# Late products with the low part of h, memory tokens scaled by ScalarE, and h of the next norm made during the last output unit

## The chip, the cores and the metric

The kernel runs on one core of one Trainium2 chip. The metric is the device time of one execution in microseconds (us). Before the change the median of three runs is 2518.27 us.

## The reference, cut to what matters

One decoder layer, for 1024 tokens of width 1024:

```python
x = x + 0.5 * swiglu(rmsnorm(x, g1), w_gu1, w_down1)          # FFN 1
h = rmsnorm(x, g_mix)
q_sb, k_sb, v_sb, q_d, k_d, v_d, q_x, gates = split(h @ w_in)
mn = rmsnorm(mem, g_mem);  mk, mv = split(mn @ w_mem_kv)      # 256 memory tokens
o_sb, o_dil, o_x = stick_breaking(...), dilated(...), memory_attention(q_x, mk, mv)
merged = g0 * (o_sb @ w_br_sb) + g1 * (o_dil @ w_br_dil) + g2 * (o_x @ w_br_x)
x = x + merged @ w_out
x = x + 0.5 * swiglu(rmsnorm(x, g2), w_gu2, w_down2)          # FFN 2
```

The norm is y = x * rsqrt(mean(x*x) + eps) * gain. All in float32.

## The kernel before, in words

Activations lie transposed: feature on the partition, token on the free axis, in eight tiles of 128 features by 1024 tokens (`xT`, `h_hi`, `h_lo`). Every large product is made in three parts. A factor is split in a rounded high part and the rest: `h = h_hi + h_lo`, `w = w_hi + w_lo`. The product is `w_hi*h_hi + w_hi*h_lo + w_lo*h_hi`, and that of the two rests is left out.

Weights come as 196 "units" of 128x1024 in a fixed order. SP (line 459) loads a unit into one of two `raw` buffers, ScalarE copies it into `w_hi` (`split_hi`, line 519, instruction at L525), VectorE makes `w_lo` (`split_lo`, line 818, instruction at L823). There are three slots for split weights, so a unit is split up to two units ahead. The semaphores `hi_done` and `split_done` count these two steps, `unit_done` counts units that TensorE has used up.

A unit of a product over eight k tiles is `product` (line 1279): per k, and for both halves of 512 tokens, six matmuls of 128x512, four with `w_hi` and two with `w_lo`, 48 in all. With `there` it waits before each k for that tile of h. Before that wait is over, none of the six is issued.

h is made without the norm's factor: `gain_hi` on ScalarE (line 534, L536) writes `h_hi[k] = gain * xT[k]`, `gain_lo` on VectorE (line 827, L830) the rest, and the factor (`rB`) is applied when PSUM is read. For it ScalarE squares each tile (`square`, L532), GpSimd adds the squares up (L476), `norm_sum` (line 1357) sums over the partitions on TensorE, ScalarE takes Ln, Exp and Square (`rstd`, line 538), and VectorE does a Newton step (`newton_rstd`, line 834). Only then can `ffn_gate` (L851) read the first unit out of PSUM.

The order on each engine is written out by hand. The places that the change touches:

- **First stage** (lines 1426 to 1447 on TensorE, 613 to 627 on ScalarE, 989 to 1000 on VectorE). TensorE turns x tile by tile (`turn_x`, L1423), VectorE takes it out of PSUM (L987), h is made, and the first two units run side by side, tile after tile. After tile 5 VectorE scales the two blocks of memory tokens (L1000). In the iteration of the last k TensorE turns the memory tokens (L1437), VectorE puts them into `mT` (L1004), ScalarE makes `mT_hi` (L631) and VectorE `mT_lo` (L1008). `norm_sum(0)` waits for the last `mT`, as it writes the same banks of PSUM.
- **Units 4 and 7** (`gate_or_up` at lines 1459 to 1468), cut into pieces with the memory products between.
- **Entry of the projections** (line 1515), the first unit behind FFN 1.
- **Output units** (lines 1684 to 1690; L1267 on VectorE adds a finished one to x; h here is `merged`, whose rest is made at L1208 and whose high part at L792).
- **Entry of FFN 2**: ScalarE waits at line 800 until the last output unit is done and then makes all `h_hi` (lines 801 to 805), VectorE makes all `h_lo` after its last addition (line 1268), and the first unit is at line 1346.

```python
act.wait_ge(unit_done, U_OUT + DT)      # line 800
...
for m in range(DT):                     # line 1264
    split_lo(U_OUT + m + AHEAD)
    dve.wait_ge(unit_done, U_OUT + m + 1)
    nc.vector.tensor_tensor(xT[:, m, :], x_back[:, m, :], ps[:, 2 + m % 2, :], ALU.add).then_inc(x_added, 1)
for k in range(DT):
    gain_lo(2, k, 2)
```

## Time and profile before

| | us |
|---|---|
| three runs, median (lowest, highest) | 2518.27 (2513.20, 2518.75) |
| the profiled execution, its own time | 2513.74 |
| its span in the profile | 2511.90 |
| TensorE (PE) busy | 2447.6, 97% |
| VectorE (DVE) busy | 1169.4, 47% |
| ScalarE (ACT) busy | 573.8, 23% |
| GpSimd (POOL) busy | 193.6, 8% |
| mean granted TensorE clock | 0.987 of full speed |
| share of the chain that ended last: PE, DVE, ACT | 92%, 4%, 2% |

PE busy includes the time in which one matmul drains while the next already runs, so it is not a measure of work done at peak. What a stall costs is read from the idle time before an instruction and from what ended it, and what the clock costs from the granted clock of a stretch. Times in the timeline are us from the start of the span.

### The profile page before, as it was taken

Reading aid. Unit: us, or ns where it says so; the run is one execution under the profiler, and the core shown is the slowest. Engines: PE = TensorE matmul, PEld = TensorE weight load, DVE = VectorE, ACT = ScalarE, POOL = GpSimd, SP = SyncE. Lnnn points to the kernel's source line nnn. Section 1 sums busy time; section 2 is a strip of 40 time slices with the busy share of each in tenths; the row PEclk is TensorE's granted clock in tenths of the full one; section 3 lists DMA queues with packets and bytes.
Section 4 is the critical chain, followed back from the end, with each engine's and each line's share of the span. In section 5 each row is a group of like instructions: output and inputs, shape, how many; then the busy total and the mean of one; then the engine's idle time right before and its main releaser. Section 6 shows DMA issues by size and latency. Waiting matters only on the chain.

```text
span 2511.9 us, 25983 instructions
## 1 busy us (share of the span) xinstructions
PE 2447.6 (97%) x10608; PEld 1915.8 (76%) x10608; DVE 1169.4 (47%) x1193; ACT 573.8 (23%) x716; POOL 193.6 (8%) x153
## 2 busy tenths in 40 slices
PE   7999999999999999889999999999999999999998
PEld 6788888888877655446667888878788888888887
DVE  7444444444446666555632533343544444444444
ACT  5211111111114444433413311121301111111111
POOL 2000000000002454330000000001000000000000
PEclk9999999999999999999999999999999999999999
DMA  4211111111113000001012211122111111111112
GB/s 148 73 42 51 50 50 50 42 50 50 50 53 120 26 9 17 17 12 39 26 28 25 59 51 51 51 91 77 42 42 51 50 50 50 42 50 50 50 50 67
DMA packets 48946, 125.80 MB, mean 50 GB/s; under 512 B 4269, under 2 KB 22605, under 8 KB 48624
## 3 DMA queue, kind: packets, MB, share of 16 engines
q1 hardware_dynamic: 45760, 112.69, 14.8%
q10 hardware_dynamic: 2640, 11.08, 1.2%
q0 software_dynamic: 480, 1.10, 0.3%
q8 instruction: 48, 0.79, 0.1%
q14 instruction: 18, 0.15, 0.0%
HBM read 116.42 MB, written 9.87 MB: 50 GB/s over the span
## 4 chain that ended last, share of the span: by engine, by line
PE 92%; DVE 4%; ACT 2%; issue 1%; DMA 0%; SPq 0%; ACTq 0%; DVEq 0%
PE ps L1277 91%; DVE h_lo L830 1%; DVE w_lo L823 0%; PE ps L1616 0%; ACT pr_x L590 0%; ACT pr_x L592 0%; DVE xT L892 0%; PE ps L1563 0%; DMA x_nat<-in_x 0%; DVE d_qk L960 0%; DVE pr_x L952 0%; DVE d_qk L955 0%; DVE h_lo L1208 0%; ACT pr_x L594 0%; PE ps L1405 0%
## 5 line engine op out<-in xcount | busy, mean ns | idle before, releaser
L1277 PE MATMUL ps<-h_hi,w_hi 128*128 128x512 f32 x2240 | 894.1, 399 | 15.7 <-DVE h_lo L830 6.6
L1277 PE MATMUL ps<-h_lo,w_hi 128*128 128x512 f32 x2240 | 878.3, 392 | 0.0
L1277 PE MATMUL ps<-h_hi,w_lo 128*128 128x512 f32 x2240 | 695.2, 392 | 0.0
L1277 PEld LDWEIGHTS ps<-h_hi,w_hi 128*128 128x128 f32 x2240 | 423.6, 189 | 136.7 <-issue 40.5
L1277 PEld LDWEIGHTS ps<-h_hi,w_lo 128*128 128x128 f32 x2240 | 423.0, 189 | 89.7
L1277 PEld LDWEIGHTS ps<-h_lo,w_hi 128*128 128x128 f32 x2240 | 424.2, 189 | 85.4 <-issue 1.9
L525 ACT ACTIVATE w_hi<-raw 128x1024 fp32r<-128x1024 f32 x196 | 204.2, 1051 | 825.6 <-PE ps L1277 799.7
L823 DVE TENSOR_TENSOR w_lo<-raw,w_hi 128x1024 fp32r<-128x1024 f32 x196 | 254.3, 1305 | 154.1 <-ACT w_hi L525 144.4
L892 DVE TENSOR_TENSOR xT<-xT,ps 128x1024 f32<-128x1024 f32 x176 | 214.7, 1220 | 182.7 <-PE ps L1277 182.7
L1277 PE MATMUL ps<-a_hi,w_hi 128*128 128x512 f32 x704 | 276.6, 393 | 5.7 <-DVE w_lo L823 4.9
L1277 PE MATMUL ps<-a_lo,w_hi 128*128 128x512 f32 x704 | 275.6, 391 | 0.0
L1277 PE MATMUL ps<-a_hi,w_lo 128*128 128x512 f32 x704 | 218.1, 391 | 0.0
L858 DVE SCALAR_TENSOR_TENSOR glu<-ps,rB 128x1024 f32<-128x1024 f32 x44 | 53.9, 1224 | 262.4 <-PE ps L1277 262.4
L851 DVE TENSOR_TENSOR silu<-ps,rB 128x1024 f32<-128x1024 f32 x44 | 53.9, 1224 | 252.1 <-PE ps L1277 252.1
L1277 PEld LDWEIGHTS ps<-a_hi,w_hi 128*128 128x128 f32 x704 | 133.0, 189 | 35.1 <-DVE w_lo L823 5.7
L1277 PEld LDWEIGHTS ps<-a_hi,w_lo 128*128 128x128 f32 x704 | 132.8, 189 | 27.8
L1277 PEld LDWEIGHTS ps<-a_lo,w_hi 128*128 128x128 f32 x704 | 133.1, 189 | 27.4
L556 ACT ACTIVATE silu<-silu 128x1024 f32<-128x1024 f32 x44 | 46.6, 1060 | 439.7 <-DVE silu L851 439.7
L476 POOL TENSOR_TENSOR acc<-acc,sq 128x1024 f32<-128x1024 f32 x21 | 51.3, 2442 | 1108.0 <-ACT sq L532 1108.0
L1150 DVE TENSOR_TENSOR gate<-ps,rB 128x1024 f32<-128x1024 f32 x24 | 29.4, 1225 | 126.5 <-PE ps L1277 126.5
L1277 PE MATMUL ps<-sb_q,sb_k 64*128 64x512 f32 (+2 forms) x144 | 62.5, 542 | 17.4 <-ACT sb_a L697 16.0
L760 ACT ACTIVATE gate<-gate 128x1024 f32<-128x1024 f32 x24 | 25.0, 1057 | 172.7 <-DVE gate L1150 172.6
(186 smaller groups left out, 1786.1 us busy)
## 6 DMA issues: line engine op xcount, KB each, us to landing
raw<-in_weights SPq DMA_DIRECT2D x196, 512.0 KB, 3.6
x_nat<-in_x SPq DMA_DIRECT2D x8, 512.0 KB, 7.4
x_keep<-xT ACTq DMA_DIRECT2D x1, 4096.0 KB, 12.6
x_back<-x_keep ACTq DMA_DIRECT2D x1, 4096.0 KB, 12.2
out<-y_nat SPq DMA_DIRECT2D x8, 512.0 KB, 3.3
toe_keep<-toe_row ACTq DMA_DIRECT2D x2, 704.0 KB, 6.6
m_nat<-in_mem SPq DMA_DIRECT2D x1, 1024.0 KB, 8.2
d_fB<-d_f_keep POOLq DMA_DIRECT2D x2, 512.0 KB, 7.3
```

What stands on the lines that cost most here:

```text
L476: nc.gpsimd.tensor_tensor(acc[:], acc[:], sq[:, k % 2, :], ALU.add).then_inc(acc_done, 1)
L525: nc.scalar.activation(w_hi[:, k % NW].rearrange("p a b -> p (a b)"), raw[:, k % NRAW, :], ACT.Copy).then_inc(hi_done, 1)
L556: nc.scalar.activation(silu[:, t % 2, :], silu[:, t % 2, :], ACT.Silu).then_inc(silu_done, 1)
L760: nc.scalar.activation(gate_tile(m, b), gate_tile(m, b), ACT.Sigmoid).then_inc(gate_done, 1)
L823: nc.vector.tensor_tensor(w_lo[:, k % NW].rearrange("p a b -> p (a b)"), raw[:, k % NRAW, :], w_hi[:, k % NW].rearrange("p a b -> p (a b)" ...
L830: nc.vector.scalar_tensor_tensor(out=h_lo[:, k, :], in0=xT[:, k, :], scalar=g32[:, gain, k:k + 1], in1=h_hi[:, k, :].bitcast(F32), op0=ALU ...
L851: nc.vector.tensor_tensor(silu[:, t % 2, :], ps[:, 0, :], rB[:], ALU.mult).then_inc(gate_scaled, 1)
L858: nc.vector.scalar_tensor_tensor(out=glu[:, t % 2, :], in0=ps[:, 1, :], scalar=0.5, in1=rB[:], op0=ALU.mult, op1=ALU.mult).then_inc(up_sca ...
L892: nc.vector.tensor_tensor(xT[:, m, :], xT[:, m, :], ps[:, 2 + m % 2, :], ALU.add).then_inc(down_added, 1)
L1150: nc.vector.tensor_tensor(gate_tile(m, b), ps[:, merge_pair(m, b), :], rB[:], ALU.mult).then_inc(mg_taken, 1)
L1277: return pe.matmul(o, a, b, start=start, stop=stop, skip_group_check=True)
```

## The change

- In the first unit of a stage, products with `h_lo` are no longer issued tile by tile with the others. A new `streamed` waits per k for `h_hi` alone, issues the four matmuls with `h_hi`, and issues the two with `h_lo` of k - 2 after them. It takes the place of `product` with `there` in the first unit of the projections, in the first output unit and in the first unit of FFN 2.
- In the first stage the wait for `h_hi` moves ahead of `turn_x(k + 2)`, the eight matmuls with `h_hi` come before the wait for `h_lo`, and for k = 0 part of them come before the turn of the third x tile. ScalarE splits weight unit 1 before it squares tile 0.
- Units 4 and 7 (`gate_or_up_part`) wait for `hi_done` only, issue what needs `w_hi`, then wait for `split_done` and issue what needs `w_lo`.
- The memory tokens are scaled by ScalarE after tile 6, no longer by VectorE after tile 5.
- In the last output unit each k but the last increments a new semaphore `out_read` as soon as its matmuls are through. ScalarE makes `h_hi[k]` of the next norm as soon as `out_read` allows, VectorE makes `h_lo[0..4]` before it waits for that unit, and `h_lo[5..7]` after its addition. The last square comes before the eighth `h_hi`, no longer before the fourth.

```diff
@@ ScalarE, first stage
                 gain_hi(k, 0)
-                square(0, k)
                 if k == 0:
                     split_hi(1)
+                square(0, k)
...
+                if k == 6:
+                    act.wait_ge(m_rs_done, 2)
+                    for b in range(MB):
+                        nc.scalar.activation(m_nat[:, b, :], m_nat[:, b, :], ACT.Copy, scale=m_rs[:, b:b + 1]).then_inc(m_scaled, 1)
@@ ScalarE, entry of FFN 2
-            act.wait_ge(unit_done, U_OUT + DT)
             for k in range(DT):
-                if k == 3:
+                if k < DT - 1:
+                    act.wait_ge(out_read, k + 1)
+                else:
                     act.wait_ge(x_added, DT)
                     square(2, DT - 1)
                 gain_hi(k, 2)
@@ VectorE, first stage
-                if k == 5:
-                    dve.wait_ge(m_rs_done, 2)
-                    for b in range(MB):
-                        nc.vector.tensor_scalar(m_nat[:, b, :], m_nat[:, b, :], m_rs[:, b:b + 1], None, ALU.mult).then_inc(m_scaled, 1)
@@ VectorE, output units
-                dve.wait_ge(unit_done, U_OUT + m + 1)
+                if m < DT - 1:
+                    dve.wait_ge(unit_done, U_OUT + m + 1)
+                if m == DT - 1:
+                    for k in range(5):
+                        gain_lo(2, k, 2)
+                    dve.wait_ge(unit_done, U_OUT + m + 1)
                 nc.vector.tensor_tensor(xT[:, m, :], x_back[:, m, :], ps[:, 2 + m % 2, :], ALU.add).then_inc(x_added, 1)
-            for k in range(DT):
+            for k in range(5, DT):
                 gain_lo(2, k, 2)
@@ TensorE, new helpers
+            def high_high(pair, slot, k):
+                for c in (0, 512):
+                    mm(ps[:, pair, c:c + 512], w_hi[:, slot, k, :], h_hi[:, k, c:c + 512], k == 0, False)
+            def rest_high(pair, slot, k, final=False):
+                for c in (0, 512):
+                    last = mm(ps[:, pair, c:c + 512], w_lo[:, slot, k, :], h_hi[:, k, c:c + 512], False, final)
+                return last
+            def high_rest(pair, slot, k, final=False):
+                for c in (0, 512):
+                    last = mm(ps[:, pair, c:c + 512], w_hi[:, slot, k, :], h_lo[:, k, c:c + 512], False, final)
+                return last
+            def streamed(pair, slot, hi_done_of, lo_done_of, base):
+                for k in range(DT + 2):
+                    if k < DT:
+                        pe.wait_ge(hi_done_of, base + k + 1)
+                        high_high(pair, slot, k)
+                        rest_high(pair, slot, k)
+                    if k >= 2:
+                        pe.wait_ge(lo_done_of, base + k - 1)
+                        last = high_rest(pair, slot, k - 2, k == DT + 1)
+                return last
...
+            def gate_or_up_part(part, k, t, k0, k1):
+                if k0 == 0:
+                    pe.wait_ge(hi_done, k + 1)
+                    after(pe, (gate_scaled, up_scaled)[part], t)
+                for j in range(k0, k1):
+                    high_high(part, k % NW, j)
+                    high_rest(part, k % NW, j)
+                if k0 == 0:
+                    pe.wait_ge(split_done, k + 1)
+                for j in range(k0, k1):
+                    last = rest_high(part, k % NW, j, j == DT - 1)
@@ TensorE, first stage
             for k in range(DT):
+                pe.wait_ge(h_hi_done, k + 1)
+                if k == 0:
+                    pe.wait_ge(hi_done, 1)
+                    high_high(0, 0, 0)
+                    pe.wait_ge(split_done, 1)
+                    rest_high(0, 0, 0)
                 if k + 2 < DT:
                     turn_x(k + 2)
...
+                if k == 0:
+                    pe.wait_ge(hi_done, 2)
+                    high_high(1, 1, 0)
+                    pe.wait_ge(split_done, 2)
+                    rest_high(1, 1, 0)
+                else:
+                    for part in range(2):
+                        high_high(part, part, k)
+                    for part in range(2):
+                        rest_high(part, part, k)
                 pe.wait_ge(h_ready, k + 1)
                 for part in range(2):
-                    if k == 0:
-                        pe.wait_ge(split_done, part + 1)
-                    last = product(part, part, hh, hl, S, k0=k, k1=k + 1)
+                    last = high_rest(part, part, k, k == DT - 1)
@@ TensorE, output units
-                product(2 + m % 2, u % NW, hh, hl, S, there=(lambda k: pe.wait_ge(mg_split, k + 1)) if m == 0 else None
-                        ).then_inc(unit_done, 1)
+                if m == 0:
+                    last = streamed(2, u % NW, mg_hi_done, mg_split, 0)
+                else:
+                    last = product(2 + m % 2, u % NW, hh, hl, S, read=out_read if m == DT - 1 else None)
+                last.then_inc(unit_done, 1)
```

## Rows read from the trace of the kernel before

**Rows 1.** The page, busy us (share of the span) and instructions of each engine.

```profile
PE 2447.6 (97%) x10608; PEld 1915.8 (76%) x10608; DVE 1169.4 (47%) x1193; ACT 573.8 (23%) x716; POOL 193.6 (8%) x153
```

**Rows 2.** Waits of PE, whole span: waited for, us in total, times, longest.

```profile
PE ps L1277 <- DVE w_lo L823: 8.3, 4, 2.4
PE ps L1277 <- DVE h_lo L830: 6.6, 3, 2.7
PE ps L1277 <- DVE h_lo L1208: 2.2, 1, 2.2
```

**Rows 3.** Stretches: us, busy (x) of PE, PEld, DVE, ACT, POOL, granted clock, DMA.

```profile
40.00:45.00 5.00, 5.00 (x20) 3.99 (x20) 3.72 (x2) 1.59 (x2) 2.53 (x1) 0.66 0.00 0
60.00:90.00 30.00, 28.89 (x143) 24.50 (x144) 14.79 (x22) 10.21 (x12) 0.00 (x0) 0.94 0.30 94
785.00:812.00 27.00, 25.17 (x106) 19.85 (x106) 10.83 (x10) 7.11 (x7) 0.00 (x0) 1.00 0.61 233
1689.00:1701.00 12.00, 12.00 (x47) 9.62 (x46) 2.42 (x3) 2.23 (x2) 0.00 (x0) 0.86 0.73 314
1771.00:1784.00 13.00, 11.94 (x46) 9.58 (x47) 11.05 (x8) 7.82 (x8) 2.87 (x1) 0.87 0.01 1
```

**Rows 4.** Timeline, first stage: start, us, engine, instructions [idle before, releaser].

```profile
29.56 1.03 PE L1423 MATMUL ps<-cst,x_nat 128*128 128x128 f32 x8
30.42 2.41 POOL L476 TENSOR_TENSOR acc<-acc,sq 128x1024 f32<-128x1024 f32 x1 [1.20 <-ACT sq L532]
31.77 2.14 DVE L830 SCALAR_TENSOR_TENSOR h_lo<-xT,g,h_hi 128x1024 fp32r<-128x1024 f32 x1
33.22 1.04 PE L1423 MATMUL ps<-cst,x_nat 128*128 128x128 f32 x8
33.83 3.54 DVE L1000 TENSOR_SCALAR m_nat<-m_nat,small 128x1024 f32<-128x1024 f32 x2
...
38.55 1.15 ACT L536 ACTIVATE h_hi<-xT,g 128x1024 fp32r<-128x1024 f32 x1 [4.56 <-DVE xT L987]
...
39.76 0.50 PE L1277 MATMUL ps<-h_hi,w_hi 128*128 128x512 f32 x1 [2.74 <-DVE h_lo L830]
```

**Rows 5.** Timeline, from the memory tokens to unit 4.

```profile
41.63 2.70 DVE L823 TENSOR_TENSOR w_lo<-raw,w_hi 128x1024 fp32r<-128x1024 f32 x1 [0.61 <-ACT w_hi L525]
...
45.30 3.23 DVE L1004 TENSOR_SCALAR mT<-ps,g 128x256 f32<-128x256 f32 x8 [0.97 <-PE ps L1437]
...
50.06 0.68 PE L1277 MATMUL ps<-mT_hi,w_hi 128*128 128x256 f32 x1
...
57.71 1.22 DVE L851 TENSOR_TENSOR silu<-ps,rB 128x1024 f32<-128x1024 f32 x1
...
60.12 0.50 PE L1277 MATMUL ps<-h_hi,w_hi 128*128 128x512 f32 x1 [2.42 <-DVE w_lo L823]
```

**Rows 6.** Timeline, start of unit 7.

```profile
77.25 0.50 PE L1277 MATMUL ps<-h_hi,w_hi 128*128 128x512 f32 x1 [1.00 <-DVE w_lo L823]
```

**Rows 7.** Timeline, last k of the first projection unit.

```profile
785.80 0.50 PE L1277 MATMUL ps<-h_hi,w_hi 128*128 128x512 f32 x1 [1.18 <-DVE h_lo L830]
```

**Rows 8.** Timeline, seventh k of the first output unit.

```profile
1687.82 1.06 ACT L792 ACTIVATE h_hi<-merged 128x1024 fp32r<-128x1024 f32 x1 [7.75 <-DVE merged L1229]
1688.60 0.50 PE L1277 MATMUL ps<-h_hi,w_hi 128*128 128x512 f32 x1 [2.16 <-DVE h_lo L1208]
```

**Rows 9.** Timeline, last output unit and entry of FFN 2.

```profile
1758.57 1.22 DVE L1267 TENSOR_TENSOR xT<-x_back,ps 128x1024 f32<-128x1024 f32 x1 [5.01 <-PE ps L1277]
...
1761.86 2.57 DVE L823 TENSOR_TENSOR w_lo<-raw,w_hi 128x1024 fp32r<-128x1024 f32 x1 [2.07 <-ACT w_hi L525]
...
1769.45 3.23 ACT L536 ACTIVATE h_hi<-xT,g 128x1024 fp32r<-128x1024 f32 x3 [7.62 <-PE ps L1277]
...
1772.06 0.76 PE L1277 MATMUL ps<-h_hi,w_hi 128*128 128x512 f32 x1 [2.65 <-DVE h_lo L830]
...
1784.64 1.88 PE L1277 MATMUL ps<-acc,cst 128*128 128x512 f32 x4
```

More of the change, by code:

```diff
@@ L340, in layer @@
         br_done = sem("br_done")
-        mg_hi_done, mg_split = sem("mg_hi_done"), sem("mg_split")
+        mg_hi_done, mg_split, out_read = sem("mg_hi_done"), sem("mg_split"), sem("out_read")
         x_added = sem("x_added")
@@ L1277, in mm, with product @@
                 return pe.matmul(o, a, b, start=start, stop=stop, skip_group_check=True)
-            def product(pair, slot, hi, lo, width, tiles=DT, w0=0, there=None, k0=0, k1=None):
+            def product(pair, slot, hi, lo, width, tiles=DT, w0=0, there=None, k0=0, k1=None, read=None):
                 halves = [(c, min(c + 512, width)) for c in range(0, width, 512)]
@@ L1290, in product @@
                         last = mm(ps[:, pair, c:d], w_lo[:, slot, w0 + k, :], hi(k)[:, c:d], False, final)
+                    if read is not None and k < tiles - 1:
+                        last.then_inc(read, 1)
+                return last
[19 more added lines that the diff above has]
+                        last = high_rest(pair, slot, k - 2, k == DT + 1)
                 return last
@@ L1345, in ffn @@
                 if f:
-                    gate_up(u0, t0, there=lambda k: pe.wait_ge(h_ready, 8 * r + k + 1), between=lambda: norm_sum(r))
+                    gate_up(u0, t0, between=lambda: norm_sum(r))
                     for q in range(1, GT):
@@ L1382, in proj @@
                         pe.wait_ge(pr_final, aux_before(before))
+                if n == PR_SB:
+                    streamed(proj_pair(n), proj_unit(n) % NW, h_hi_done, h_ready, 8).then_inc(unit_done, 1)
+                    return
                 last = product(proj_pair(n), proj_unit(n) % NW, hi, lo, w, there=there, k0=k0, k1=k1)
@@ L1406, in proj_aux, with projections @@
                     last.then_inc(pr_aux, 1)
-            def projections(n0, n1, hi, lo, there=None):
+            def projections(n0, n1, hi, lo):
                 for n in range(n0, n1):
-                    proj(n, hi, lo, there if n == n0 else None)
+                    proj(n, hi, lo)
                     if n == n0:
@@ L1513, in sb_values @@
                 last.then_inc(sb_av, 1)
-            projections(PR_SB, PR_BESIDE, hh, hl, lambda k: pe.wait_ge(h_ready, 8 + k + 1))
+            projections(PR_SB, PR_BESIDE, hh, hl)
             pe.wait_ge(pr_copied, PR_BESIDE)
```

26 lines of the change are left out of this document (15 added, 11 removed).

## The prediction

> **What bounds the kernel now.** I read the busy times first: TensorE is busy 97% of the span, no other engine over 47% [rows 1]. So time is only to be had where TensorE stands, or where it runs at half its clock. The view of its waits shows where it stands. Most lie in the attention stages, which the change leaves alone. Three groups are its targets [rows 2]: 6.6 us for `h_lo` of the norms in three waits, 2.2 us for that of the merged tiles in one, and 8.3 us for `w_lo` in four, of which two (2.42 and 1.00) belong to units 4 and 7 [rows 5, 6].
>
> The third view is the clock by stretch [rows 3]. 40 to 45 us has 0.66, 60 to 90 us 0.94, 1689 to 1701 us 0.86, 1771 to 1784 us 0.87. Length times what is missing from 1.00 gives 1.70, 1.8, 1.68 and 1.69 us: each is one stretch of about 3.4 us at 1.2 instead of 2.4 GHz, which costs 1.7 us. Before each TensorE had stood idle: 2.74, 2.42, 2.16 and 2.65 us [rows 4, 5, 8, 9]. After the idle 1.18 us of rows 7 the clock stayed at 1.00. So a stall of over 2 us costs its length plus 1.7 us, one of 1.2 us only its length. That is the price list of this prediction.
>
> The pace of matmuls at full clock: an output unit is 48 matmuls and runs from 1758.5 to 1769.4 us [rows 9] (both ends are marked by what PE released), 10.9 us or 0.227 us each, 1.36 us per k.
>
> **The first stage, up to the norm's sum.** From turn to turn TensorE takes 3.66 us (29.56 to 33.22) [rows 4], all busy. Then VectorE spends 3.54 us on the memory tokens, its second scaling held up by GpSimd's addition, as the subtraction at 31.77 is (2.14 us for some 1.2, ending 1.1 us after GpSimd's 30.42 + 2.41). `h_lo` 6 is late, and TensorE stands 2.74 us and then loses 1.70.
>
> ScalarE takes the scaling over: two Copies of 128x1024, of which a row with a scale costs 1.08 us (3.23 for three) [rows 9], so 2.1 us. It stood idle 4.56 us for the last x tile here [rows 4], so they are hidden; they push `h_hi` 7 to about 37 us, which TensorE wants at 38. Bounds: 0 and 2.1 us, taken as 0. No DMA is issued or moved; SP and GpSimd keep their order.
>
> VectorE now goes straight to x tile 7 (its turn ends at 33.22 + 1.04; 34.3 to 35.5), is held by GpSimd until 36.5 (one period of 3.66 after 30.42 + 2.41), ends `h_lo` 6 at 37.6 and 7 at 38.8. GpSimd's last sum then runs to 41.2 and holds `w_lo` of unit 2 to 42.2 (before: to 44.3) [rows 5]. The eight `mT` follow, 3.23 us, to 45.5. The earlier start (four matmuls move into the wait for the third x tile) may take 0.5 off this, nothing to 1.2. I take 45.3, against 48.5 before, with the norm's sum right behind it and the first memory product 1.5 us behind it (50.06) [rows 5]. **Gain 3.2 us.**
>
> TensorE's own work is done sooner than that: the turn of tile 7 began at 33.22, k = 6 would follow at 36.9, and two k (5.4 us) and sixteen turns (1.9) end at 44.2, or at 42.7 with a start that is 1.5 us earlier. The old stall of 2.74 us and its slow clock are gone, but a new one stands before the sum, of 1.2 to 2.7 us, for `mT`. I take the upper half and so a new slow stretch over the memory products: **-1.6 us** (bounds 0 and 1.7), of which nothing is hidden since memory product 0 and `rstd` end together before.
>
> **Units 4 and 7.** The chain from memory product to `rB` keeps its length. Unit 4 now needs PSUM bank 0 free, which is when L851 ends, 58.93, and no longer `w_lo`, which came at 60.1. Start 58.95 against 60.12: **1.2 us**. The stall is 1.2 instead of 2.42 us, so the clock should hold: **1.7 us**. `w_lo` is wanted 16 matmuls (3.6 us) later and is there. Unit 7 waited 1.00 us for its `w_lo`; its first eight matmuls (1.8 us) now cover that: **1.0 us** (bounds 0, if `w_hi` isn't there either, and 1.0).
>
> **Entry of the projections.** The last k waited 1.18 us for `h_lo` 7 [rows 7]. `h_hi` 7 is long there, and two matmuls are left instead of six when `h_lo` 7 arrives. The seven k before the stall took 9.5 us, so the unit began at 775.1; 46 matmuls end at 785.5, two more after 785.8. End 786.3 against 787.2: **0.9 us**. No clock was lost here.
>
> **First output unit.** Before, TensorE stood at k = 6 for `h_lo` 6 from 1686.4 to 1688.6, with 12 matmuls left (2.72 us): end 1691.3 at full clock. Now it gets through k = 6 and `h_lo` 4 (38 matmuls, 8.6 us from 1678.3) at 1686.9, and then stands for `h_hi` 7, which ends at 1688.88 [rows 8]. Ten matmuls are left, 2.27 us: end 1691.2. The stall is 2.0 us, hardly shorter, the slow stretch stays. **0.1 us.**
>
> **Entry of FFN 2.** Before, TensorE stands from 1769.4 to 1772.06, runs slowly, and reaches the norm's sum at 1784.64 [rows 9]. Now ScalarE, idle 7.62 us there, starts after its split at 1761.8: seven `h_hi` at 1.08 are done by 1769.6, none held long by `out_read` (k = 6 is read at 1768.1). VectorE is free at 1764.4, makes five `h_lo` to 1770.5 and adds tile 7 by 1771.7, 1 us later than before. ScalarE squares it to 1772.8 and has `h_hi` 7 at 1773.9; GpSimd sums to 1775.2; `h_lo` 6, held by it, ends at 1776.4, `h_lo` 7 at 1777.6. TensorE starts at 1769.45, wants `h_hi` 7 at 1778.1 and `h_lo` 7 at 1779.9. Nothing is late, the unit ends at 1769.45 + 10.9 = 1780.35. **4.3 us**, which holds the stall, the slow stretch and 0 to 0.1 of small waits. What is queued behind ScalarE's new waits is only its own h and `rstd`, and that starts with the sum.
>
> By the Trainium skill, page "TensorE: Matmul & The Clock Gate", section "The cost: per-tile semaphore tail", each semaphore increment on a matmul adds about 26 ns. The seven of `out_read` would then take an estimated 0.2 us off the sum. No row here shows such a step.
>
> **Sum.** 3.2 - 1.6 + 1.2 + 1.7 + 1.0 + 0.9 + 0.1 + 4.3 = **10.8 us**. Between the stages TensorE is the bound, so gains are carried on. The profiled execution took 2513.74 us (span 2511.90, 1.84 around it) and would take 2502.9. It lies 4.5 us under the median of 2518.27; from that the forecast is **2507.5 us**.
>
> **Rivals.**
> 1. *More clock than I take.* The new stall before the norm's sum is short (lower end 1.2 us), or the slow stretch at the first output unit doesn't come. Gain 12.4, with both 14.1: 2505.9 to 2504.2. For: the stall's lower end. Against: four of four idles over 2.1 us were followed by a slow stretch. Chance 0.20.
> 2. *The memory chain keeps its old time.* `mT` isn't earlier, for instance because GpSimd and VectorE hold each other up once more, 2.4 us. Then the first term is 0.8 and the sum 8.4: 2509.9. For: it hangs on three turns of GpSimd and VectorE whose order I worked out to half a microsecond. Chance 0.15.
> 3. *The last addition is late.* Five `h_lo` ahead of it, each possibly held to 2.14 us as in rows 4, would bring it to 1776 and the norm's sum to wait; of the 4.3 us some 1.5 would be left, sum 8.0: 2510.3. Against: GpSimd only adds squares there, and that of tile 7 comes after the addition. Chance 0.07.
> 4. *The new order of matmuls is slower.* The old order puts two after each other into one PSUM bank; the new ones change the bank with each matmul. It concerns 336 matmuls. If each ran at half clock, it would cost 0.2 us, 67 us in all, and the time would be about 2574; from 79 such matmuls (10.8 + 5.0 us at 0.2) the change is slower by over 0.2%. Against: a third of today's matmuls (those with `w_lo`) already change bank each time, and 785 to 812 us has clock 1.00 [rows 3]. Chance 0.04. The Trainium skill has a rule for it, page "TensorE: Matmul & The Clock Gate", section "A second HAM failure mode: psum-queue depth-cycling": cycling through banks leaves small idles that make the clock swing between its levels. The trace does not agree so far.
> 5. *Little comes of it*: 2 and 3 together, and a stall that only moved at unit 4, sum 3 to 5 us: about 2514. Chance 0.09.
>
> **How the numbers follow.** My own case has 0.45. About 0.2% (5.0 us) is what a measurement of this kernel can tell from no change. Cases 0 to 3 are faster by more: 0.87; case 5 the same: 0.09; case 4 slower: 0.04. Low end of the range: case 1 with a median that falls among the quicker of the runs (before, 2513.20 to 2518.75): 2500. High end: rivals 2 and 3 with a microsecond more: 2513. The predicted time is that of my case.
>
> **What would show it.** L1000 gone from VectorE, two more ScalarE Copies of about 1.1 us near 34 us. `mT` begun at 42.2 instead of 45.3, and a PE wait for `mT` L1004. Unit 4 released by L851, not L823, and clock 1.00 over the gate products of unit 4. No wait for `w_lo` at unit 7. A wait for `h_lo` L830 of at most 0.4 us at the projections. A wait of about 2.0 us for `h_hi` L792 and still a slow stretch at the first output unit. At FFN 2 no wait and no slow stretch, and 10.9 instead of 15.2 us from the end of the last output unit to the norm's sum. I would be wrong if TensorE's waits for h and `w_lo` shrank as told and the span did not, or if the stretches with the new order took over 0.227 us a matmul.

## The result, and the profile after

| | before | after |
|---|---|---|
| median, us | 2517.06 (2513.20 to 2518.75, 6 runs) | 2498.10 (2495.66 to 2500.43, 6 runs) |
| ratio, 95% interval | | 0.9926 (0.9913 to 0.9939) |
| profiled execution, us | 2513.74 | 2497.57 |
| its span, us | 2511.94 | 2495.67 |

The change gained 19.0 us by the medians, 16.2 us by the two profiled executions. The forecast was 10.8 us and a time of 2507.5, with a range from 2500.0: sign right, size too small, range missed.

The page after the change, engines:

```profile
PE 2439.7 (98%) x10608; PEld 1910.5 (77%) x10608; DVE 1168.8 (47%) x1191; ACT 576.0 (23%) x718; POOL 194.2 (8%) x153
```

The same 10608 matmuls, two instructions fewer on VectorE and two more on ScalarE [rows 1]. PE is busy 7.9 us less with the same work. Most of that is clock: the trace after has four stretches at half clock (1.2 instead of 2.4 GHz) fewer, at 1.7 us each. The other 8.4 us of the gain are waiting. After, the waits of PE that answer to those of before:

```profile
PE ps L1283 <- DVE w_lo L828: 5.1, 3, 2.5
...
PE ps L1283 <- ACT h_hi L796: 2.0, 1, 2.0
...
PE ps L1283 <- DVE silu L856: 1.4, 1, 1.4
PE ps L1283 <- DVE mT L1005: 1.4, 1, 1.4
...
PE ps L1283 <- DVE h_lo L835: 0.3, 1, 0.3
```

17.1 us of waiting [rows 2] became 10.2, and the x DMA at the very start costs 1.5 us less (7.6 after). The stretches that answer to [rows 3] (us, busy and instructions of PE, PEld, DVE, ACT, POOL, granted clock, DMA share, GB/s):

```profile
40.00:45.00 5.00, 3.65 (x15) 2.27 (x13) 5.00 (x15) 4.11 (x9) 0.00 (x0) 1.00 0.38 105
60.00:90.00 30.00, 30.00 (x156) 24.12 (x155) 16.52 (x22) 8.85 (x10) 0.00 (x0) 1.00 0.28 80
1678.00:1690.00 12.00, 11.11 (x42) 9.02 (x43) 2.14 (x3) 3.17 (x3) 0.00 (x0) 0.86 0.86 350
1759.00:1772.00 13.00, 13.00 (x56) 10.09 (x55) 8.14 (x6) 2.30 (x4) 3.47 (x1) 1.00 0.00 1
```

Of the four stretches at half clock that the prediction read, three are gone, and that at the first output unit stays. The timeline of the kernel after, in the same places as [rows 4 to 9]:

```profile
32.06 2.18 ACT L631 ACTIVATE m_nat<-m_nat,small 128x1024 f32<-128x1024 f32 x2
32.25 1.22 DVE L992 COPY xT<-ps 128x1024 f32<-128x1024 f32 x1
37.22 3.03 DVE L828 TENSOR_TENSOR w_lo<-raw,w_hi 128x1024 fp32r<-128x1024 f32 x1 [0.28 <-ACT w_hi L525]
40.17 3.21 DVE L1005 TENSOR_SCALAR mT<-ps,g 128x256 f32<-128x256 f32 x8
43.53 1.95 PE L1283 MATMUL ps<-acc,cst 128*128 128x512 f32 x4 [1.35 <-DVE mT L1005]
44.92 0.68 PE L1283 MATMUL ps<-mT_hi,w_hi 128*128 128x256 f32 x1
53.94 0.70 PE L1283 MATMUL ps<-h_hi,w_hi 128*128 128x512 f32 x2 [1.37 <-DVE silu L856]
68.26 0.63 PE L1283 MATMUL ps<-h_hi,w_hi 128*128 128x512 f32 x2
776.71 0.73 PE L1283 MATMUL ps<-h_lo,w_hi 128*128 128x512 f32 x2 [0.29 <-DVE h_lo L835]
1678.89 0.73 PE L1283 MATMUL ps<-h_hi,w_hi 128*128 128x512 f32 x2 [2.03 <-ACT h_hi L796]
1748.41 1.22 DVE L1273 TENSOR_TENSOR xT<-x_back,ps 128x1024 f32<-128x1024 f32 x1 [5.01 <-PE ps L1283]
1751.58 7.51 ACT L536 ACTIVATE h_hi<-xT,g 128x1024 fp32r<-128x1024 f32 x7
1754.22 6.05 DVE L835 SCALAR_TENSOR_TENSOR h_lo<-xT,g,h_hi 128x1024 fp32r<-128x1024 f32 x5
1760.20 1.20 DVE L1273 TENSOR_TENSOR xT<-x_back,ps 128x1024 f32<-128x1024 f32 x1
1769.97 1.88 PE L1283 MATMUL ps<-acc,cst 128*128 128x512 f32 x4
```

How far after is ahead of before at each landmark (the start of an instruction in the timeline of both) tells where the time came from:

| landmark | before, us | after, us | ahead by | new here |
|---|---|---|---|---|
| memory product 0 | 50.06 | 44.92 | 5.14 | 5.14 |
| unit 4 starts | 60.12 | 53.94 | 6.18 | 1.04 |
| its first four k done | 67.31 | 59.47 | 7.84 | 1.66 |
| unit 7 starts | 77.25 | 68.26 | 8.99 | 1.15 |
| norm's sum 2 | 787.29 | 777.28 | 10.01 | 1.02 |
| first output unit starts | 1678.12 | 1668.08 | 10.04 | 0.03 |
| addition of output tile 6 | 1758.57 | 1748.41 | 10.16 | 0.12 |
| norm's sum 3 | 1784.64 | 1769.97 | 14.67 | 4.51 |
| end of the span | 2511.94 | 2495.67 | 16.27 | 1.60 |

The last 1.60 us lie in code that the change doesn't touch, in the last down product of the second FFN. Both kernels stand there 2.45 us for `w_lo`. The same stretch of the two (8 us from just ahead of that stall in before, 8 us around it in after):

```profile
2470.00:2478.00 8.00, 5.55 (x18) 4.15 (x17) 2.90 (x3) 1.06 (x1) 0.00 (x0) 0.80 0.01 2
```

```profile
2458.00:2466.00 8.00, 6.22 (x27) 5.18 (x28) 3.39 (x4) 0.43 (x1) 0.00 (x0) 1.00 0.00 0
```

Before is the first fence and after the second: the same stall, followed by half clock in one and by full clock in the other. What is behind that became the question of the experiments, beside the size of the first term.

### The profile page after: what moved, and what is told of

It is laid out like the page before. It is cut to its first block, busy times and chain, and to the rows that moved or that the text cites. A ratio compares the mean times of both kernels' runs of the same rounds, so it can differ in the third digit from the quotient of the medians.

```text
span 2495.7 us, 25983 instructions
## 1 busy us (share of the span) xinstructions
PE 2439.7 (98%) x10608; PEld 1910.5 (77%) x10608; DVE 1168.8 (47%) x1191; ACT 576.0 (23%) x718; POOL 194.2 (8%) x153
## 4 chain that ended last, share of the span: by engine, by line
PE 92%; DVE 4%; ACT 2%; issue 1%; DMA 0%; SPq 0%; ACTq 0%; DVEq 0%
PE ps L1283 91%; DVE h_lo L835 1%; DVE w_lo L828 0%; PE ps L1687 0%; ACT pr_x L590 0%; ACT pr_x L592 0%; DVE xT L897 0%; PE ps L1634 0%; DVE d_qk L965 0%; DVE pr_x L957 0%; DVE d_qk L960 0%; ACT pr_x L594 0%; PE ps L1462 0%; PE ps L1774 0%; DMA x_nat<-in_x 0%
## 5 line engine op out<-in xcount | busy, mean ns | idle before, releaser
L1283 PE MATMUL ps<-h_hi,w_hi 128*128 128x512 f32 x2240 | 880.7, 398 | 6.9 <-DVE d_qk L965 3.5
L1283 PE MATMUL ps<-h_lo,w_hi 128*128 128x512 f32 x2240 | 865.3, 391 | 0.3 <-DVE h_lo L835 0.3
L856 DVE TENSOR_TENSOR silu<-ps,rB 128x1024 f32<-128x1024 f32 x44 | 53.9, 1224 | 252.1 <-PE ps L1283 252.1
```

The costliest lines, as they stand in the source:

```text
L856: nc.vector.tensor_tensor(silu[:, t % 2, :], ps[:, 0, :], rB[:], ALU.mult).then_inc(gate_scaled, 1)
L1283: return pe.matmul(o, a, b, start=start, stop=stop, skip_group_check=True)
```

## The experiments

There were three groups of four, each with its own runs of the kernel before (medians 2516.12, 2517.95 and 2516.15 us). The code shown is shortened to the lines that matter. Every ratio is to those, with its 95% interval. Kernels of a group can be compared with each other directly. First, parts of the change put into the kernel before.

### The memory tokens alone

```diff
-                if k == 5:
-                    dve.wait_ge(m_rs_done, 2)
-                    for b in range(MB):
-                        nc.vector.tensor_scalar(m_nat[:, b, :], ...)
+                if k == 6:
+                    act.wait_ge(m_rs_done, 2)
+                    for b in range(MB):
+                        nc.scalar.activation(m_nat[:, b, :], ..., ACT.Copy, scale=...)
```

> The kernel before with one part of the change: ScalarE scales the memory tokens after tile 6. In the changed kernel the first memory product began at 44.92 us, 5.14 earlier than before, where 3.2 was forecast. Theory (head start): the surplus comes from TensorE's earlier work on k = 0, which moves every turn of x and so VectorE's chain; then this part alone gives what the prediction worked out without it, first memory product at 46.4 to 47.1 us, x tile 7 taken at about 34.3. Rival (slack): the chain behind the scaling was shorter than worked out, and the product begins at 45.4 or sooner with this part alone. Both expect the wait of 2.74 us for h_lo gone and no slow clock at 41 us.

Measured: 2512.72 us (10 runs), 0.9984 (0.9975 to 0.9994). From its timeline:

```profile
29.88 1.22 DVE L991 COPY xT<-ps 128x1024 f32<-128x1024 f32 x1 [0.30 <-PE ps L1423]
...
33.58 1.23 DVE L991 COPY xT<-ps 128x1024 f32<-128x1024 f32 x1 [0.38 <-PE ps L1423]
...
44.62 1.96 PE L1277 MATMUL ps<-acc,cst 128*128 128x512 f32 x4 [0.20 <-DVE mT L1004]
```

The memory product follows the sum at 46.01, 4.05 us ahead of before's 50.06. Not all of this is the edit's. The copies of x tile 6, which lies ahead of anything that was edited in this kernel, in before (first fence) and after (second):

```profile
30.63 1.22 DVE L987 COPY xT<-ps 128x1024 f32<-128x1024 f32 x1 [0.32 <-PE ps L1423]
```

```profile
28.71 1.21 DVE L992 COPY xT<-ps 128x1024 f32<-128x1024 f32 x1
```

Tile 6 was copied at 30.63 in before and at 29.88 here: this execution was 0.75 us ahead by its first turns alone. From that copy to the memory product it takes 16.13 us against 19.43 before, **3.3 us** for moving the scaling. In after it is 16.21 us. So the 5.14 us of the full change are 3.22 behind tile 6's copy, which moving the scaling alone gives as well, and 1.92 ahead of it. About 1.0 of the 3.3 us is half clock that before's profiled execution had behind its stall of 2.74 us; the entry of FFN 2 alone, below, shows this. The expectation had the product at 46.4 to 47.1 us, the rival at 45.4 or sooner: 46.01 lies between them, and would be some 46.8 without the 0.75 us. With a wait of only 0.20 us in front of the sum there is no stretch at half clock.

### The order of the first stage, without and with its head start

Both kernels build on the last one. The first has `h_lo`'s products at the end of each k; the second has beside that what the change does at k = 0, of which the first five added lines are the part for unit 0 (products of `w_hi` and `w_lo` 0 and 1 spread around the turns, and ScalarE's `split_hi(1)` ahead of its square).

```diff
+                if k == 0:
+                    pe.wait_ge(hi_done, 1)
+                    high_high(0, 0, 0)
+                    pe.wait_ge(split_done, 1)
+                    rest_high(0, 0, 0)
                 if k + 2 < DT:
                     turn_x(k + 2)
...
+                for part in range(2):
+                    high_high(part, part, k)
+                for part in range(2):
+                    rest_high(part, part, k)
                 pe.wait_ge(h_ready, k + 1)
                 for part in range(2):
-                    last = product(part, part, hh, hl, S, k0=k, k1=k + 1)
+                    last = high_rest(part, part, k, k == DT - 1)
```

> As mem_alone, and in the first stage the products with the low part last in each k, but nothing of k = 0 before the turn of the third x tile and no change of the order on ScalarE. Theory (head start): no earlier than mem_alone by over 0.5 us, since from k = 1 on TensorE is the bound and the order within a k changes no sum. Rival (order within k): the late products with h_lo alone bring 1.5 us or more, first memory product at 45.4 or sooner.

> As mem_alone, with the whole new order of the first stage (k = 0 begins before the turn of the third x tile, weight unit 1 split before square 0); units 4 and 7 as before. Theory (head start): first memory product at 44.9 us as in the changed kernel, 1.5 to 2.1 earlier than mem_alone, x tile 7 taken at 32.3. Rival (slack): same time as mem_alone. Time of the run: 5.1 us under the kernel before for the shift and 1.7 for the slow stretch at 61 us only if it does not stay.

Measured: 2513.01 us, 0.9988 (0.9979 to 0.9998), and 2511.10 us, 0.9977 (0.9968 to 0.9987), 10 runs each. The norm's sum in the one without the head start:

```profile
44.87 1.96 PE L1277 MATMUL ps<-acc,cst 128*128 128x512 f32 x4 [1.19 <-DVE mT L1004]
```

and in the one with it, with the start of unit 4:

```profile
43.52 1.96 PE L1277 MATMUL ps<-acc,cst 128*128 128x512 f32 x4 [1.35 <-DVE mT L1004]
...
54.98 0.50 PE L1277 MATMUL ps<-h_hi,w_hi 128*128 128x512 f32 x1 [2.41 <-DVE w_lo L827]
```

The late `h_lo` within a k gives the chain nothing: tile 6 is copied at 30.14, and the memory product follows 16.12 us later, as in the kernel with the scaling alone. The head start shows in the copy of tile 6, at 28.64: 1.5 us earlier than 30.14, 1.2 than 29.88. Of that 1.35 and 1.1 are left at the memory product (44.91 against 46.26 and 46.01). So of the 1.92 us that after has at this copy some 1.2 to 1.5 are the edit's and 0.4 to 0.7 are where the profiled execution of before lay. Unit 4, with its old product, still stands 2.41 us for `w_lo`.

### The entry of FFN 2 alone

ScalarE's waits for `out_read`, the five `h_lo` ahead of the last addition and the increments on the last output unit go into the kernel before; the product of the first FFN unit stays the old one, six matmuls a k.

```diff
-            act.wait_ge(unit_done, U_OUT + DT)
             for k in range(DT):
-                if k == 3:
+                if k < DT - 1:
+                    act.wait_ge(out_read, k + 1)
+                else:
                     act.wait_ge(x_added, DT)
```

> The kernel before with the new entry of FFN 2 alone, but with the old product in the first unit of FFN 2, which waits for h_lo before each k. As predicted for the change: 2.65 us of stall and 1.7 of slow clock gone, 4.3 to 4.5 us from the end of the last output unit to the norm's sum, 4.3 in all. Theory: h made early is the whole of it, and the products two k behind bring nothing here as h_lo 7 would be late by at most 0.5 us. Rival: without them TensorE waits for h_lo 6 and 7, which are held by GpSimd, and only 2 to 3 us are won.

Measured: 2511.64 us (10 runs), 0.9983 (0.9973 to 0.9992). Its timeline has two lines of the first stage, which is that of before, then the addition of output tile 6 and the norm's sum:

```profile
39.76 0.50 PE L1281 MATMUL ps<-h_hi,w_hi 128*128 128x512 f32 x1 [2.73 <-DVE h_lo L831]
...
49.02 0.68 PE L1281 MATMUL ps<-mT_hi,w_hi 128*128 128x256 f32 x1
...
1758.84 1.22 DVE L1271 TENSOR_TENSOR xT<-x_back,ps 128x1024 f32<-128x1024 f32 x1 [5.00 <-PE ps L1281]
...
1780.40 1.88 PE L1281 MATMUL ps<-acc,cst 128*128 128x512 f32 x4
```

From addition to sum it takes 21.56 us, against 26.07 before and 21.56 after. The whole gain of this part thus comes from making h early. That `h_lo`'s products come two k late, which the change also does here, adds nothing.

The first of these lines is the more telling. The stall is that of [rows 4], 2.73 us instead of 2.74 at the same 39.76, and the clock behind it:

```profile
35.00:47.00 12.00, 9.27 (x49) 7.44 (x47) 11.36 (x12) 5.28 (x9) 4.37 (x2) 1.00 0.12 29
```

1.00, where before has 0.66 over 40 to 45 us. The norm's sum comes at 47.63 instead of 48.70, the memory product at 49.02 instead of 50.06, with tile 6 copied at 30.63 in both. The same instructions with the same stall kept full clock in this execution: the price list of the prediction isn't a rule. It also tells what the 3.3 us above hold: against this execution the scaling alone saves 18.39 - 16.13 = 2.3 us, and the other 1.0 is the half clock that went with the stall. The stall of unit 4 (2.42 us, at 59.08) was followed by full clock here too.

### Parts of the change taken back: units 4 and 7, and the streamed units

The second group starts from the kernel after. In the first of these two, `gate_or_up_part` is the old product, six matmuls a k behind a wait for `w_lo`; in the second, `streamed`, which serves the first units of the projections, of the output stage and of FFN 2, is the old product.

```diff
             def gate_or_up_part(part, k, t, k0, k1):
                 if k0 == 0:
-                    pe.wait_ge(hi_done, k + 1)
+                    pe.wait_ge(split_done, k + 1)
                     after(pe, (gate_scaled, up_scaled)[part], t)
-                for j in range(k0, k1):
-                    high_high(...); high_rest(...)
...
+                last = product(part, k % NW, hh, hl, S, k0=k0, k1=k1)
```

> The changed kernel with units 4 and 7 as before (wait for split_done, old order). Both sides of the prediction's term: 1.2 us at the start of unit 4 and 1.0 at unit 7 come back as waits for w_lo of 2.4 and 1.0 us; and the stretch at half clock behind the first, 1.7 us, if it comes with every stall over 2 us. By the profile of the changed kernel the term was 1.04 + 1.66 + 1.15 = 3.9 us. Rival: unit 7's start hides behind something else and only 1.0 to 1.7 us come back.

```diff
             def streamed(pair, slot, hi_done_of, lo_done_of, base):
+                return product(pair, slot, hh, hl, S,
+                               there=lambda k: pe.wait_ge(lo_done_of, base + k + 1))
```

> The changed kernel with the old product (waits for h_lo before each k) in the first unit of the projections, the first output unit and the first unit of FFN 2. By the terms: 0.9 us comes back at the projections, 0.1 at the output units, nothing at FFN 2, where h_lo is early; 1.0 us in all. Rival: the late products with h_lo are worth more than the waits show (they also spare TensorE's clock), and 2.5 us or more come back.

Measured: 2502.80 us (4 runs), 0.9944 (0.9928 to 0.9961) without the new units 4 and 7, and 2501.17 us (4 runs), 0.9937 (0.9921 to 0.9954) without the streamed ones. The first one's timeline at the two units:

```profile
56.06 0.50 PE L1283 MATMUL ps<-h_hi,w_hi 128*128 128x512 f32 x1 [2.41 <-DVE w_lo L828]
...
73.22 0.50 PE L1283 MATMUL ps<-h_hi,w_hi 128*128 128x512 f32 x1 [1.00 <-DVE w_lo L828]
```

Both waits are back, and with the first of them the clock of 0.83:

```profile
55.00:65.00 10.00, 8.94 (x32) 7.19 (x33) 6.03 (x8) 3.52 (x7) 0.00 (x0) 0.83 0.49 135
```

The norm's sum 1 lies at 44.61 in this execution, 1.08 us later than in after (an x tile landed later, and TensorE stood 2.11 instead of 1.27 us for it), and the toe (the narrow matmuls of the bias table behind unit 7, `TOE_KINDS`) starts at 87.70 instead of 82.66. Of these 5.04 us 1.08 were there before, so 3.96 belong to the two units. The prediction gave them 3.9. In the second kernel the stall at the projections is back:

```profile
775.70 0.50 PE L1283 MATMUL ps<-h_hi,w_hi 128*128 128x512 f32 x1 [1.18 <-DVE h_lo L835]
```

0.9 us more than the 0.29 of after. More half clock, near 802 and 1027 us, came with this execution in code that is that of after: 0.66 over 800 to 815 us against 1.00, and 0.66 over 1025 to 1040 against 0.82. It makes this execution 5.7 us longer between the sum 2 and the last attention block than after was. That is more than the part that was taken back, and no reading of a size can be made from its total; the rival of 2.5 us or more isn't ruled out by it.

### The stall at the last down product

Outside the attention stages and the wait for the first x tiles, the two largest waits left are at both FFNs' last down product, where TensorE stands for the `w_lo` of its second unit. Here the first unit's products of tiles 0 and 1 are issued ahead of that wait.

```diff
-                down(g0 + NGRP - 1, u0 + FFN_UNITS - GT, 0, finish=finish)
+                down_last(g0 + NGRP - 1, u0 + FFN_UNITS - GT, 0, finish=finish)
...
+                pe.wait_ge(split_done, k + 1)
+                for m in range(2):
+                    pe.wait_ge(down_added, DT * g + m - 1)
+                    half(m, 0)
+                pe.wait_ge(split_done, k + GT)
+                for m in range(DT):
+                    if m >= 2:
+                        pe.wait_ge(down_added, DT * g + m - 1)
+                        half(m, 0)
+                    last = half(m, 1)
```

> The changed kernel, and in the last down product of each FFN the parts of the first two output tiles that need only the first of its two weight units are issued before the wait for w_lo of the second (24 matmuls become issuable of which 12 lie before the wait, 2.7 us). The changed kernel stands 2.45 us there in each FFN (at 740.68 and 2459.78 us) and was at half clock after the first of the two and not after the second. Theory (every stall is paid at its length, the clock on top by chance): both waits go, 4.9 us from the stalls and 0 to 3.4 from the clock, 1.7 on average: ratio to the kernel before near 0.990, some 6 us under the changed kernel. Rival: the second down unit's w_lo then holds the additions of VectorE, and the stall moves to the waits for the sums of tiles 0 and 1: 0 to 2 us won.

Measured: 2493.89 us (4 runs), 0.9907 (0.9890 to 0.9923). The waits of PE that it changes:

```profile
PE ps L1283 <- DVE xT L897: 1.2, 3, 0.5
PE ps L1283 <- DVE w_lo L828: 0.4, 1, 0.4
```

5.1 us of waiting for `w_lo` became 0.4, at the price of 0.4 more for `xT`. From the toe to the norm's sum 2 it takes 688.6 us, where after took 692.1, and from the norm's sum 3 to the first output tile taken from PSUM 696.9 instead of 699.2. The first difference, 3.5 us, holds the stall and the stretch at half clock behind it; the second, 2.2, the stall alone, which after had at full clock.

### The stalls moved by 2.4 us

The matmuls of the toe are issued twice (the second time over the same result). That puts all that follows 2.4 us later and changes nothing else; once on the kernel after, once on that of before.

```diff
-            for g, _, _, w, c in TOE_KINDS:
+            for g, _, _, w, c in TOE_KINDS + TOE_KINDS:
                 last = mm(...)
```

> The changed kernel with the five small matmuls of the bias table issued twice (same output), so that TensorE has about 2.4 us more work near 85 us and all behind it is moved by that much, with every stall as long as before. Theory A (a stall of 2.0 to 2.5 us is followed by half clock or not, depending on when it falls): the stretches at half clock behind the stalls at 740, 1679 and 2460 us come or stay away otherwise than in the changed kernel's profile, and the time is 2.4 us plus a small multiple of 1.7, up or down. Theory B (length of the stall alone decides): the same stretches as in the changed kernel, each moved by 2.4 us, and the time is up by 2.4 us.

> The kernel before with the small matmuls of the bias table twice: 2.4 us more work. Theory A (chance of position): segments with the same code differ from those of the kernel before by steps of about 1.7 us (bias table to second sum 693.0, second sum to the last sb_a 336.2, third sum to the first y_nat 700.8 in its profile), so that the time is not simply 2.4 us up. Theory B (length of stall alone): all segments the same, time up by 2.4 us.

Measured: 2501.76 us (4 runs), 0.9944 (0.9927 to 0.9960), and 2519.49 us (10 runs), 1.0014 (1.0005 to 1.0024). In the shifted kernel after, the stretches behind the two stalls for `w_lo`, of 2.45 us both:

```profile
740.00:748.00 8.00, 5.55 (x18) 4.06 (x17) 2.62 (x3) 3.29 (x3) 0.00 (x0) 0.79 0.75 194
2459.00:2467.00 8.00, 7.43 (x26) 5.94 (x27) 1.77 (x3) 0.00 (x0) 0.00 (x0) 0.79 0.00 0
```

Both are slow; in after only the first was (0.79 over 739 to 747). In the shifted kernel before:

```profile
90.00:102.00 12.00, 12.00 (x39) 6.35 (x38) 5.99 (x7) 1.06 (x1) 0.00 (x0) 0.72 0.06 12
...
813.00:823.00 10.00, 7.27 (x27) 4.80 (x26) 4.88 (x8) 2.34 (x5) 0.34 (x1) 0.83 0.00 0
```

and the two stretches in before that answer to them:

```profile
88.00:100.00 12.00, 12.00 (x52) 8.36 (x51) 6.99 (x8) 1.06 (x1) 0.00 (x0) 1.00 0.15 37
...
809.00:819.00 10.00, 7.28 (x35) 5.15 (x33) 4.88 (x8) 3.18 (x7) 0.34 (x1) 1.00 0.01 2
```

PE is busy 7.28 and 7.27 us in the later pair, so its idle time is the same (stalls of 1.32 and 1.41 us), but one runs at 1.00 and the other at 0.83. Slow stretches can so appear behind stalls that didn't change. Whether the shift does it or chance, these two runs can't tell; the next one does.

### The kernel after once more

No edit. If the clock behind a stall followed from the kernel, a second profiled execution would show the same stretches.

> The changed kernel itself, once more, beside the next two and on the same chip. Theory A (half clock behind a stall comes or stays away by where the stall falls, and the runs spread by it): the landmarks up to the first norm's sum, the bias table and the second sum agree with the first profile within 0.5 us, and what differs lies in steps of about 1.7 us in the stretches behind stalls (740, 800 to 1130, 2460 us). Rival: the surplus over the forecast belongs to the first set of runs (another chip), and the ratio is nearer to 0.995.

Measured: 2498.87 us (5 runs), 0.9932 (0.9918 to 0.9945), in line with the first measurement: 17.3 us against this group's runs of before, where the first measurement had 19.0. The rival, that the surplus over the forecast belonged to the first set of runs, is out. Timeline, the first FFN's last down product:

```profile
740.83 0.50 PE L1283 MATMUL ps<-a_hi,w_hi 128*128 128x512 f32 x1 [2.45 <-DVE w_lo L828]
```

Its windows:

```profile
739.00:747.00 8.00, 6.17 (x27) 5.13 (x28) 3.39 (x4) 4.56 (x5) 0.00 (x0) 1.00 0.85 228
797.00:807.00 10.00, 7.27 (x29) 5.10 (x28) 4.66 (x8) 1.95 (x4) 0.34 (x1) 0.84 0.00 0
```

and the same of the first execution of after:

```profile
739.00:747.00 8.00, 6.32 (x21) 5.05 (x22) 2.85 (x3) 2.98 (x4) 0.00 (x0) 0.79 0.87 238
797.00:807.00 10.00, 7.27 (x35) 5.38 (x34) 3.25 (x6) 1.96 (x4) 0.00 (x0) 1.00 0.01 2
```

One kernel, two executions, the same stalls to 0.01 us, and the slow stretch changed its place: slow at 740 and not at 800 in the one, the other way round in the other. So it isn't fixed by the kernel. From toe to sum 2 the new execution took 690.5 us (1.6 less), from there to the last attention block 338.9 (2.7 more).

How often half clock follows a stall can be counted over all 14 profiled executions, before, after and the twelve experiments, outside the attention stages except for the pair near 800 us:

| stall of TensorE | length, us | executions that have it | followed by half clock |
|---|---|---|---|
| first stage, for `h_lo` 6 | 2.73 to 2.75 | 3 | 2 |
| unit 4, for `w_lo` | 2.41 to 2.42 | 7 | 6 |
| last down product of FFN 1 | 2.45 | 12 | 8 |
| pair near 800 us | 1.32 and 1.41 | 14 | 8 |
| first output unit | 2.03 to 2.16 | 12 | 12 |
| entry of FFN 2 | 2.65 | 5 | 5 |
| last down product of FFN 2 | 2.45 | 12 | 10 |
| single stalls of 0.99 to 1.40, all places | 0.99 to 1.40 | 33 | 0 |

So a single stall of 2.0 to 2.8 us was followed by half clock 43 times in 51, and one of 1.0 to 1.4 us never.

### The first output unit, and the best of both

The stall of 2.03 us for `h_hi` 7 is what the new order left. `x_back`'s transfer is issued by ScalarE ahead of that h, and TensorE waits for it with products of `h_lo` 5 still unissued behind it.

```diff
-                if m == DT - 1:
-                    act.dma_start(x_back[...], x_keep[:, :]).then_inc(x_back_in, 16)
                 nc.scalar.activation(h_hi[:, m, :], merged_tile(m), ACT.Copy).then_inc(mg_hi_done, 1)
+                if m == DT - 1:
+                    act.dma_start(x_back[...], x_keep[:, :]).then_inc(x_back_in, 16)
...
+                    for k in range(DT + 2):
+                        if k >= 2:
+                            pe.wait_ge(mg_split, k - 1)
+                            last = high_rest(2, u % NW, k - 2, k == DT + 1)
+                        if k < DT:
+                            pe.wait_ge(mg_hi_done, k + 1)
+                            high_high(2, u % NW, k)
+                            rest_high(2, u % NW, k)
```

> The changed kernel; in the first output unit the two products with h_lo of k - 2 stand ahead of the wait for h_hi of k, and ScalarE issues the transfer of x_back behind the last high part of the merged tiles instead of ahead of it. The stall of 2.03 us there becomes one of about 1.2 (0.45 less from the two products, 0.35 from the issue). Theory: 0.8 us off, and 1.7 more where the clock now holds. Rival: h_hi 7 is not any earlier as it waits for the merged tile, 0.45 us only and the clock as before.

> after_mg and after_last_down together: their gains add, some 5 to 8 us under the changed kernel, ratio to the kernel before near 0.990. Rival: gains overlap and it is no faster than after_last_down.

Measured: 2495.88 us (5 runs), 0.9922 (0.9908 to 0.9935) for this edit; with that of the last down products as well 2492.01 us (2487.49 to 2493.15, 4 runs), 0.9902 (0.9886 to 0.9917), against 2498.87 for the kernel after in the same group. Timeline of the first of the two:

```profile
1676.87 0.73 PE L1283 MATMUL ps<-h_hi,w_hi 128*128 128x512 f32 x2 [1.20 <-ACT h_hi L794]
...
1690.56 0.47 PE L1283 MATMUL ps<-h_hi,w_hi 128*128 128x512 f32 x1 [0.68 <-DVE xT L1273]
```

The stall went from 2.03 to 1.20 us, and this execution has clock 1.00 over 1676 to 1688, but the later transfer makes the addition of tile 0 late: a new wait of 0.68 us takes most of the shortened stall back. The 3.0 us between this kernel and after (2498.87) aren't clear of noise, as their intervals overlap. The version with both edits beats both kernels, before by 24.1 us and after by 6.9 us.

## Why the prediction was wrong

The miss is 9.4 us (2507.5 against 2498.1). **It breaks down so:** 5.4 us are in the profiles (16.2 instead of 10.8), 2.8 us in where the two profiled executions lie (before's 3.3 us under its median, after's 0.5), and 1.2 us in before's median, 2518.27 from three runs and 2517.06 from six.

Of the 5.4 us, 1.9 are the first term, 1.6 the term of -1.6 us that didn't come, and 1.6 the stretch at 2475 us; 0.3 are small differences of the others.

**The steps that failed are two: the clock taken as fixed, and the sizes of the first stage.** "A stall over 2 us costs its length plus 1.7 us, one of 1.2 us only its length" was read from five stalls of one execution. The size holds: a slow stretch costs up to 1.7 us (1.66 at unit 4). As a rule it doesn't hold. Single stalls of 2.0 to 2.8 us were followed by half clock in 43 of 51 cases, so the mean price is about 1.4 us, an estimate from this count. Those of 2.73 (the entry of FFN 2 alone, at 39.76) and 2.45 us (after at 2459.78, and again at 740.83) went by at clock 1.00, and a pair of 1.32 and 1.41 was followed by 0.84. Of the 5.4 us, 1.6 are such a stretch that before's execution had at 2475 us and after's hadn't. The prediction had no term for it: no part of the change is there. That it fell on this side is chance.

**The term of -1.6 us failed by the length of its stall.** The new stall before the norm's sum is 1.35 us. The prediction had its bounds (1.2 to 2.7) right, took the upper half and put half clock behind it; over 40 to 45 us the clock is 1.00. By its own price list 1.35 us cost no clock. `mT` ended at 43.4 us instead of 45.3, while TensorE's own work ended at 42.2, a little before the 42.7 that was the early bound. Rival 1 held exactly this, with 0.20.

**The first term was mis-sized:** 3.2 us for a memory chain whose end came 5.14 us earlier. Behind tile 6's copy it was 3.2 us shorter, where the prediction had 3.0 (48.5 less 45.5), and ahead of it 1.9, where its sum had 0.2: the text gives the head start 0.5, but 45.5 went to 45.3 only. The prediction let VectorE be held by GpSimd until 36.5, then `h_lo` 7 end at 38.8 and `w_lo` at 42.2. In fact x tile 7 was taken at 32.25 instead of 34.3, both `h_lo` ran from 33.39 to 36.9, and `w_lo` ended at 40.25. The 2.0 us at tile 7 are the head start, whose bounds were 0 to 1.2 (1.2 to 1.5 found in the turns), and 0.4 to 0.7 of difference between the first turns of two executions, which the prediction had no term for. The holding by GpSimd was there as told (3.54 us for two `h_lo`, 3.03 for `w_lo`), so rival 2, a further 2.4 us of it, is out. That the part behind tile 6 came out right is in part luck: about 1.0 of it is the half clock behind before's old stall, which another execution of the same first stage didn't have.

**The offset from own time to median failed as a step.** "It lies 4.5 us under the median of 2518.27; from that the forecast is" takes the place of one execution in the spread as fixed. It is what the slow stretches happened to be in that execution. The range should have had this on both sides: 2500.0 was the low end, 1.9 us too high.

**What held.** Units 4 and 7: 1.2 + 1.7 + 1.0 = 3.9 forecast; 1.04 + 1.66 + 1.15 = 3.85 in the landmarks, 4.0 by taking them back. Unit 4 was released by `silu` L856 after 1.37 us, as told. Projections: 0.9 forecast, a wait of 0.29 left, 0.90 gained in the unit. First output unit: 0.1 forecast, 0.12 from its start to the addition of tile 6, with the wait for `h_hi` of 2.03 and clock 0.86 as told. Entry of FFN 2: 4.3 forecast, 4.51 measured, 10.9 us from the end of the last output unit to the sum as told; but the streamed products have no share in it. The seven `h_hi` and five `h_lo` ended at 1759.1 and 1760.3 in good time, so rival 3 (last addition late) is out, the addition being at 1760.20. The ScalarE copies took 2.18 us from 32.06, hidden. The medians of ten runs agree with the profiles for two parts put into before: 5.0 us for the first stage with its head start, 4.5 us for the entry of FFN 2.

**Rival 4** (the new order of matmuls is slower) is out: the 48 matmuls of the first unit of FFN 2 take 10.88 us (1759.09 to 1769.97), 0.227 us each, and 1759 to 1772 has clock 1.00. The rule of the Trainium skill, page "TensorE: Matmul & The Clock Gate", section "A second HAM failure mode: psum-queue depth-cycling", isn't borne out in this order of banks.

The estimate of 0.2 us for seven increments isn't borne out either: the last two matmuls of the unit that carries them start 10.23 us behind the addition of tile 6 with the increments (1758.64) and without (1768.80 in before). The Trainium skill, page "TensorE: Matmul & The Clock Gate", section "The cost: per-tile semaphore tail", gives its 26 ns for the increments of several tiles, which it says serialize; here one comes per k, 1.36 us apart.

## What to carry to other kernels

When stalls shrink, count what TensorE waits for and what of it is certain, the stall's own length. Treat the half clock behind it as a chance with a price. Here a single stall of 2.0 to 2.8 us had it in 43 of 51 cases at up to 1.7 us, one of 1.0 to 1.4 us never, and two of 1.3 and 1.4 us close together in 8 of 14. It isn't a fixed part, since it moves between executions of one kernel. A sum made against one profiled execution must be set against the median with that spread in the range, and slow stretches in code that the change leaves alone belong in it. And when one part is tried alone, measure it from the last event ahead of the edit, and ask what of the old time was clock: the memory chain seemed to gain 4.05 us, of which 0.75 were there before the edited code began and 1.0 was half clock behind the old stall.

## What was not expected of the hardware

- **The clock behind a stall isn't repeatable.** In two executions of one kernel the same stall of 2.45 us at 740.7 and 740.8 us was followed by 0.79 and by 1.00, and the pair of 1.3 and 1.4 us at 800 us by 1.00 and by 0.84. What decides it no run here shows: the moment in the run, or something outside the kernel. At the first output unit it followed all twelve stalls of 2.03 to 2.16 us, and no reason for that is shown either. The kernels' runs spread by about 5 us (2495.66 to 2500.43; 2513.46 to 2518.89), about three such stretches, and the mean granted clock goes with the time: 0.990 in the run of 2495.66 us, 0.988 in that of 2500.43.
- **A slow stretch came with no stall in front.** In the kernel before with the toe's matmuls doubled PE is busy throughout 90 to 102 us and the clock is 0.72; in after with the same doubling it is 1.00 over 80 to 90 and over 84 to 96. In both, 5 us of narrow matmuls (33 partitions, 256 columns) lie ahead. It is one more place where the same work had both clocks.
- **A copy out of PSUM wasn't held up by GpSimd.** In the kernel after, `h_lo` (tensor sources in SBUF) took 2.30 us beside GpSimd's addition, against 1.27 us in before at 12.97 us with GpSimd idle, and the copy of x tile 7 out of PSUM 1.22 us beside the next addition. `w_lo`, from two SBUF sources, took 3.03 us, against 1.22 with GpSimd idle.
